# Second attention of a two-block transformer kernel: the queries' norm left out of the rotation and put into the exponentials and the row maxima, the norm weights put into tables and copies, and the first two score groups issued earlier

## What is computed

```python
qkv = u @ w_in
q = qkv[..., :1024].reshape(B, S, 16, 64)
k = qkv[..., 1024:1280].reshape(B, S, 4, 64)
v = qkv[..., 1280:].reshape(B, S, 4, 64)
q = partial_rope_2(rms_norm_2(q, q_gain), cos, sin)
k = partial_rope_2(rms_norm_2(k, k_gain), cos, sin)
scores = einsum(q, k) * (64 ** -0.5)            # masked to the window
probs = softmax(concat([scores, sink]))[..., :-1]
out = einsum(probs, v).reshape(B, S, 1024) @ w_out
```

## Time and profile before

| | |
|---|---|
| median of 3 runs | 1316.03 us (1315.31 to 1316.38) |
| profiled execution, its own time | 1316.13 us |
| its span | 1314.3 us |
| busy: PE / DVE / ACT / POOL | 98% / 75% / 55% / 8% of the span |
| second attention, projection and groups | about 545.5 to 609.6 us of the span |

### The profile page before, as it was taken

How to read it: one execution, slowest core, us unless ns; L and a number is a source line. 1 busy time by engine, 2 the same in 40 slices (tenths; PEclk the granted TensorE clock), 3 DMA queues, 4 the chain that set the end, 5 groups by cost and what they waited for, 6 DMA issues and landing times.

```text
span 1314.3 us, 21966 instructions
## 1 busy us (share of the span) xinstructions
PE 1291.2 (98%) x8296; PEld 1144.0 (87%) x8296; DVE 980.7 (75%) x1628; ACT 727.7 (55%) x1175; POOL 100.9 (8%) x95
## 2 busy tenths in 40 slices
PE   7999999999999999999999999999999999999998
PEld 6888889998888888987888888899998888888887
DVE  6866677767687666787776666899887975766666
ACT  5444446656554444675665555677653545655553
POOL 1000000000000000130000000013202820000000
PEclk9999999999999999999999999999999999999999
DMA  8655555720365555323355555454431123555552
GB/s 302 210 204 187 188 185 177 256 97 1 113 210 206 191 191 192 131 95 129 133 188 191 191 191 192 161 164 165 163 120 65 66 94 131 193 192 191 191 192 96
DMA packets 30600, 214.80 MB, mean 163 GB/s; under 512 B 3648, under 2 KB 3776, under 8 KB 5184
## 3 DMA queue, kind: packets, MB, share of 16 engines
q1 hardware_dynamic: 30096, 212.23, 45.9%
q0 software_dynamic: 432, 1.57, 0.4%
HBM read 212.74 MB, written 1.05 MB: 163 GB/s over the span
## 4 chain that ended last, share of the span: by engine, by line
PE 89%; DVE 6%; ACT 2%; issue 2%; DMA 1%; POOL 0%; SPq 0%; POOLq 0%; DVEq 0%; ACTq 0%
PE bank L508 25%; PE bank L669 24%; PE bank L503 19%; PE bank L705 5%; PE bank L496 5%; PE bank L884 1%; PE bank L934 1%; PE bank L903 1%; DVE w_lo L2216 1%; ACT w_hi L1486 1%; DVE aT L2451 1%; PE bank L561 1%; PE bank L1125 1%; DMA raw<-weights 1%; PE bank L1360 0%
## 5 line engine op out<-in xcount | busy, mean ns | idle before, releaser
L2216 DVE TENSOR_TENSOR w_lo<-raw,w_hi 128x2048 fp32r<-128x2048 f32 x151 | 348.6, 2310 | 110.9 <-ACT w_hi L1486 110.5
L1486 ACT ACTIVATE w_hi<-raw 128x2048 fp32r<-128x2048 f32 x198 | 377.9, 1910 | 69.1 <-PE bank L508 34.7
L669 PE MATMUL bank<-aT,w_hi 128*128 128x512 f32 x1424 | 340.4, 390 | 0.7 <-DVE aT L2243 0.6
L669 PEld LDWEIGHTS bank<-aT,w_hi 128*128 128x128 f32 x1424 | 263.6, 188 | 54.5 <-DVE aT L2243 1.4
L508 PEld LDWEIGHTS bank<-aT,w_lo 128*128 128x128 f32 x1664 | 212.4, 191 | 7.0
L508 PE MATMUL bank<-aT,w_lo 128*128 128x256 f32 x1664 | 215.9, 283 | 0.0
L503 PE MATMUL bank<-w_hi,hT_hi 128*128 128x512 f32 x400 | 156.5, 391 | 0.0
L508 PE MATMUL bank<-w_lo,hT_hi 128*128 128x512 f32 x400 | 151.9, 389 | 0.0
L705 PE MATMUL bank<-w_hi,hT_lo 128*128 128x512 f32 x322 | 125.3, 389 | 0.0
L503 PE MATMUL bank<-w_hi,aT 128*128 128x256 f32 (+1 forms) x736 | 119.0, 313 | 0.4 <-DVE aT L2243 0.2
L2224 DVE TENSOR_TENSOR w_lo<-raw,w_hi 128x1024 fp32r<-128x1024 f32 x95 | 115.5, 1218 | 1.6 <-ACT w_hi L1486 1.6
(11 more groups left out here) (395 smaller groups left out, 1730.7 us busy)
## 6 DMA issues: line engine op xcount, KB each, us to landing
raw<-weights SPq DMA_DIRECT2D x198, 1024.0 KB, 4.9
post_gain<-post_gains POOLq DMA_DIRECT2D x3, 512.0 KB, 4.2
residual<-x SPq DMA_DIRECT2D x2, 512.0 KB, 4.0
raw<-weights SPq DMA_DIRECT2D x2, 512.0 KB, 7.3
out<-residual SPq DMA_DIRECT2D x2, 512.0 KB, 2.6
par<-params SPq DMA_DIRECT2D x1, 809.0 KB, 11.1
con<-consts SPq DMA_DIRECT2D x1, 520.0 KB, 11.1
con<-consts SPq DMA_DIRECT2D x1, 64.0 KB, 4.2
```

Source lines behind the costliest of these rows:

```text
L669: nc.tensor.matmul(to[part][:, :], w, aT[:, k, :, :].rearrange("p a c -> p (a c)"), start=k == 0, stop=False)
L1486: nc.scalar.activation(w_hi[:, i % 3, :], raw[:, i % 3, :], ACT.Copy).then_inc(w_hi_done, 1)
L2216: nc.vector.tensor_tensor(w_lo[:, i % 3, :], raw[:, i % 3, :], w_hi[:, i % 3, :].bitcast(f32), ALU.subtract).then_inc(w_lo_done, 1)
```

## The change

Six edits, all for the second attention:

- The norm weights of queries and keys are no longer a pass over the block (L2665 is gone). For the 16 rotated dimensions they are multiplied into the sine and cosine tables once (eight small DVE operations in `set_up_tables`, results in `gain_tables`); for the others they become the per-partition factor of the copy of the transposed heads (`copy_heads` takes `scale` from `P("qk_column")` in place of a constant; two memsets put 1 at the rotated dimensions, a third operation puts the 1/8 in).
- The queries are rotated without their own norm: the pass L2667 stays for the keys alone.
- The norm is applied later: each exponential takes the query's norm as its per-partition `scale` (beside the bias), and each row maximum is multiplied by it (a new small DVE operation in `maximum`).
- PE issues score groups 0 and 1 inside item 5, and its low products for t = 1 and the last two transposes behind them.
- ACT takes the exponentials of group 0 ahead of `copy_block` of the values, and copies heads 1 and 2 earlier, on either side of the square of block 3.
- DVE takes the maximum of group 0 ahead of the last rotation.

```diff
@@ PE, attention_projection
-                project_rows(i, 5, 0)
+                high_rows(i, 5, 0)
                 turn_heads("att_in", 2, [3, 7])
-                project_rows(i, 5, 1).then_inc(item_done, 1)
+                low_ready(i)
+                low_rows(i, 5, 0, False)
                 pe.wait_ge(heads_copied, 10)
                 pe.wait_ge(copied, 15)
                 scores("att_in", 0)
+                high_rows(i, 5, 1, False)
+                pe.wait_ge(copied, 16)
+                scores("att_in", 1)
+                low_rows(i, 5, 1).then_inc(item_done, 1)
                 turn_heads("att_in", 3, [3, 7])
                 turn_heads("att_in", 4, [3, 7])
-
-                pe.wait_ge(copied, 16)
-                scores("att_in", 1)
                 pe.wait_ge(heads_copied, 12)
                 pe.wait_ge(copied, 17)
@@ ACT, copy_heads
+                scale = scales[b]
+                if layer == "att_in":
+                    scale = P("qk_column")[:, b == 0:(b == 0) + 1]
...
-                    nc.scalar.activation(heads[:, at:at + 2, :], source, ACT.Copy, scale=scales[b])\
+                    nc.scalar.activation(heads[:, at:at + 2, :], source, ACT.Copy, scale=scale)\
@@ ACT, attention_projection
                     if p == 5:
-                        copy_heads("att_in", 2, [3, 7])
+                        exponentials("att_in", 0)
                     copy_block("att_in", i, p, block)
+                    if p == 4:
+                        copy_heads("att_in", 1, [3, 7])
...
+                        if p == 4:
+                            copy_heads("att_in", 2, [3, 7])
                         split(i + 3)
-                    if p in (3, 4):
-                        copy_heads("att_in", p - 3, [3, 7])
+                    if p == 3:
+                        copy_heads("att_in", 0, [3, 7])
                 copy_heads("att_in", 3, [3, 7])
                 copy_heads("att_in", 4, [3, 7])
-                exponentials("att_in", 0)
                 exponentials("att_in", 1)
@@ ACT, exponentials
+                                                scale=query_rstd_column(n, c) if layer == "att_in" else 1.0,
@@ DVE, attention_projection
-                        gain = P("qk_gain")[:, 64 * (block == 4):64 * (block == 4) + 64]
-                        link(nc.vector.tensor_tensor(v, v, spread(spread(gain, 4, 1), 2, 1), ALU.mult))
-                        dve.wait_ge(head_normed, p)
-                        link(nc.vector.tensor_tensor(v, v, spread(r, 64, 3), ALU.mult))
-                        rope(block, cos_sin[:, 0:2, :], cos_sin[:, 2:4, :])
-                maximum("att_in", 0)
+                        if p == 1:
+                            dve.wait_ge(head_normed, 1)
+                            link(nc.vector.tensor_tensor(v, v, spread(r, 64, 3), ALU.mult))
+                        at = 16 * (block == 4)
+                        rope(block, [gain_tables[:, a, at:at + 16].rearrange("p (t c) -> p t c", t=2) for a in range(4)])
+                    if p == 4:
+                        maximum("att_in", 0)
                 maximum("att_in", 1)
@@ DVE, maximum
+                    if n in (0, 2):
+                        dve.wait_ge(head_normed, 3 + n)
+                    r = query_rstd(n)
+                    link(nc.vector.tensor_tensor(to.rearrange("p (j b) -> p j b", j=2) if count == 4 else to,
+                                                 to.rearrange("p (j b) -> p j b", j=2) if count == 4 else to, r, ALU.mult))
                     last = nc.vector.tensor_tensor(to, to, neg_sinks[:, h0:h0 + count], ALU.min)
@@ DVE, set_up_tables
+                cos, sin = cos_sin[:, 0:2, :], cos_sin[:, 2:4, :]
+                for side in range(2):
+                    gain = P("qk_gain")[:, 64 * side:64 * side + 16]
+                    for a, (angle, g) in enumerate(((cos, gain[:, 0:8]), (sin, gain[:, 8:16]),
+                                                    (cos, gain[:, 8:16]), (sin, gain[:, 0:8]))):
+                        nc.vector.tensor_tensor(gain_tables[:, a, 16 * side:16 * side + 16].rearrange("p (t c) -> p t c", t=2),
+                                                angle, spread(g, 2, 1), ALU.mult)
+
+                for rows in (slice(0, 16), slice(64, 80)):
+                    last = nc.vector.memset(P("qk_column")[rows, :], 1.0)
+                link(last)
+                nc.vector.tensor_scalar(P("qk_column")[:, 0:1], P("qk_column")[:, 0:1], 0.125, None, ALU.mult)
```

More of the change, by code:

```diff
@@ L33 @@
 LEVELS = [32, 64]
-PARAMS = {"gains": 56, "subln": 1, "gdn_norm": 1, "gdn_conv": 128, "ffn_conv": 144, "ffn_bias": 48, "a_log": 16,
+PARAMS = {"gains": 56, "subln": 1, "gdn_norm": 1, "qk_column": 2, "gdn_conv": 128, "ffn_conv": 144, "ffn_bias": 48, "a_log": 16,
           "dt_bias": 16, "pe": 32, "w2k": 256, "w2v": 128, "lambdas": 256, "qk_gain": 128, "sinks": 16, "small": 448}
@@ L169, in two_blocks @@
         used[0] = shared_at
+        gain_tables = rot[:, :, 192:224]
         v_pad = room(2, 2, 320)
@@ L398, in nsa_scale, with query_rstd, query_rstd_column @@
             return P("subln") if k < 4 else C("ones")[:, 0:1]
+        def query_rstd(n):
+            t, h0, count = GROUPS["att_in"][n]
+            r = head_rstd.rearrange("p (b t j a) -> p b t j a", b=5, t=2, j=2)[:, :, t, :, h0 // 4 % 2]
+            r = r[:, 1 + h0 // 8 * 2:3 + h0 // 8 * 2, :].rearrange("p b j -> p j b")
+            return r if count == 4 else r[:, h0 % 4 // 2, :]
+        def query_rstd_column(n, c):
+            t, h0, _ = GROUPS["att_in"][n]
+            q = HEADS["att_in"][h0 + c][0]
+            at = 8 * (1 + q // 2) + 4 * t + 2 * (q % 2) + h0 // 4 % 2
+            return head_rstd[:, at:at + 1]
         def squares_of(p):
@@ L1717, in copy_heads @@
                 act.wait_ge(keys_zeroed, 1)
-                nc.scalar.activation(to[0][0:64], source[0:64], ACT.Copy, scale=scales[b])
-                nc.scalar.activation(to[1][64:128], source[64:128], ACT.Copy, scale=scales[b])\
+                low, high = (scale[0:64], scale[64:128]) if layer == "att_in" else (scale, scale)
+                nc.scalar.activation(to[0][0:64], source[0:64], ACT.Copy, scale=low)
+                nc.scalar.activation(to[1][64:128], source[64:128], ACT.Copy, scale=high)\
                     .then_inc(heads_copied, 1)
@@ L2570, in ffn, with rope @@
                 ffn_order(dve, name, tile, down)
-            def rope(b, cos, sin):
+            def rope(b, tables):
                 v = proj[:, :, 256 * b:256 * b + 256].rearrange("p t (h d) -> p t h d", d=64)
@@ L2577, in rope @@
                 parts = [rot[:, a, at:at + 64].rearrange("p (t h d) -> p t h d", t=2, d=8) for a in range(4)]
-                cos, sin = spread(cos, 4, 2), spread(sin, 4, 2)
-                for to, a, c in zip(parts, (x1, x2, x2, x1), (cos, sin, cos, sin)):
-                    last = nc.vector.tensor_tensor(to, a, c, ALU.mult)
+                for to, a, c in zip(parts, (x1, x2, x2, x1), tables):
+                    last = nc.vector.tensor_tensor(to, a, spread(c, 4, 2), ALU.mult)
                 link(last)
@@ L2605, in mixer_projection @@
                         dve.wait_ge(copied, projections(p) + 1)
-                        rope(b, table[:, 0], table[:, 1])
+                        rope(b, [table[:, 0], table[:, 1], table[:, 0], table[:, 1]])
                     if p == 0:
@@ L3241, in _parameters @@
         "gdn_norm": a["gdn_norm_2"][0].reshape(128, 1),
+        "qk_column": _np.tile(_np.stack([a["attn_q_gain_2"].reshape(64), a["attn_k_gain_2"].reshape(64)], 1), (2, 1)),
         "gdn_conv": taps(a["gdn_conv_2"][0]),
```

## The result

Nine executions of the changed kernel have their median at 1320.26 us (1318.27 to 1320.53), against 1316.03 us for the kernel before: 1.0027 times as long, 95% interval 1.0019 to 1.0036. In a second session seven more gave 1318.74 us (1318.26 to 1320.28), 1.0026 (1.0015 to 1.0037). Both medians hide that there are two groups of times with nothing between them: eight of the sixteen executions lie from 1318.26 to 1318.94, the other eight from 1319.92 to 1320.53. The kernel before shows no such pair: 107 executions from 1315.31 to 1317.31. The profiled execution took 1318.94 us (span 1317.1), from the lower group: 2.81 us more than that of before. I explain first those 2.8 us, then the second group.

A forecast was written before the change was run, and what follows sets the result against it. PE was taken to bound the kernel, with only 2.4 us of early stalls to win. Terms 1.16 + 0.10 + 0.59 + 0.39 = 2.24 us on 1316.13 gave 1318.4, less 0.1 to the median 1318.3; range 1316.2 to 1319.7.

The forecast's parts named there:

- Slower by over 0.2%: Outcome class for the whole kernel, made up of the tipping or set-up case and the table-load case: chance 0.33.
- tipping loop: Rival: costlier product and operands leave the steady ACT loop 0.13 short each two groups; +3.0, 1319.1; 0.32 with set-up.
- uncovered set-up: Rival: the tables' set-up in the feed-forward layer ahead is not hidden; +1.1, 1319.5; chance 0.32 shared with tipping.
- table load: Rival: ACT's switch between copies, exponentials and square puts one 1.28 us load on the path; 1319.6, chance 0.01.
- Group 2 starts late, second transpose 585.4, +1.16: Score group 2 waits for head copies until 580.4, 1.6 late; second transpose of exponentials moves from 584.24 to 585.4.
- Operand 0.095, product 0.20: Each per-partition operand of an ACT operation costs 0.095 us; the new small DVE product in the maximum costs 0.20.
- additions are hidden: Rival: operands and product cost nothing, only the late group 2 remains; +0.4, 1316.4, chance 0.11.
- Steady loop +0.10, half split +0.59, last group +0.39: Second attention's three later places, where the added product and operands lengthen the ACT and DVE chains by these us.
- Set-up costed at nothing: About 1.1 us of added DVE table operations in the feed-forward layer ahead, taken as covered by a full PE.
- The parameter columns: Two more columns of parameters in the first DMA, claimed to cost nothing.
- The sum as work alone: Stage terms added as lengths of work and waits: 2.24 us, with nothing behind taking it back.

The follow-up runs named there:

- order_only: Changed kernel's instruction order with the arithmetic of the kernel before (both passes back, constant scales, no product), parameter columns kept: 1316.76 us.
- no_operand: Changed kernel with the exponentials' scale left at constant 1, so without the queries' norm there: 1317.87 us.
- no_product: Changed kernel without the small DVE product in the row maximum: five of ten executions 1317.38 to 1317.85 us, five 1319.21 to 1319.74.
- layout_only: Kernel before with only the two extra parameter columns, loaded and used by nobody: 1316.71 us against 1315.98.
- long_pause: Changed kernel with two more unused ACT copies lengthening PE's wait ahead of the second transpose: 1321.06, 1321.11, 1321.12 and 1322.39 us.
- fill: Changed kernel with unused matmuls in PE's waits, 4 ahead of score group 2 and 8 ahead of the second transpose: 1318.46 us.
- mended: Changed kernel's arithmetic, last head transposes and copies early, transposed-exponentials copy ahead of exponentials n + 2, 16 parameter columns: 1314.71 us, 0.9992 of before.

## Why the prediction was right and where it was wrong

I forecast 1318.3 us, range 1316.2 to 1319.7. The median of nine, 1320.26, lies above that range; the lower group and the second session's median lie inside. Five of the nine fell in the upper group: with one fewer the median would have been 1318.94, so on which side of my bound it came out was luck. "Slower by over 0.2%" came true, and I had given it 0.33 where I gave 0.59 to no measurable difference; but those 0.33 stood for a tipping loop, an uncovered set-up and a table load, and none of the three happened.

That the lower group (median 1318.5) lies so near to 1318.3 is luck in part too: my sum of 2.24 us for the stage was 0.35 too high (1.9 measured), and a term that I had put at nothing cost 0.7.

- *Group 2 starts late, second transpose 585.4, +1.16*: group 2 began at 580.33 (forecast 580.4), the second transpose at 585.37, with waits of 1.22 and 2.21 us where I named 1.5 and 2.2. Without the 0.20 that was there before the stage the term is 0.9. What I had too high is group 2's start: PE began 0.05 us behind the end of the head copies (579.01 + 1.27 = 580.28, 580.33), where I took 0.15. Of the 0.9, the late start by itself is only 0.2 (*order_only*).
- *Operand 0.095, product 0.20*: the two-head exponential takes 0.56 us (0.47 before), the head copy 94 ns more, the product stands 0.20 ahead of the minimum. The rival "additions are hidden" is refuted by *no_operand* and *no_product*.
- *Steady loop +0.10, half split +0.59, last group +0.39*: measured 0.04, 0.56 and 0.38. The loop did not tip.
- *Set-up costed at nothing*: right (PE 22.10 of 22.10). *Table loads*: L1826 follows L1734 without one (580.15 behind 579.01 + 1.27 on ACT).
- *The parameter columns: "nothing"*: this step failed. The columns alone cost 0.7 us, shown by *layout_only*; the loss is not at the first transfer but in the gated delta layer, where GpSimd's multiplies take longer, and with 16 columns in place of 2 it is gone.
- *The sum as work alone*: this step failed too. I priced PE's waits by their length, and took one of 1.25 us to 2.2 us without asking what the clock does in it. The clock is in none of my rivals. The upper group lies about 1.8 us above the lower in half of the executions, and it moves the median out of the range.

That the clock falls in such a wait, some 2.2 us into it, is shown in the profile of *long_pause*. For the changed kernel itself no execution of the upper group was profiled; there the cause rests on *fill* and on the table of waits. The granted clock averaged over these executions (0.998 to 0.999, the lower group's 0.999 to 1.000) says little. The profiled execution is of the lower group and has 0.999 as well, and it loses that in the last 1.7 us of its span, behind the last matmul:

```profile
1315.40:1317.10 1.70, 0.00 (x0) 0.00 (x0) 0.00 (x0) 0.00 (x0) 0.00 (x0) 0.52 0.49 200
```

Open is what decides between the groups of one kernel, and which operand's address makes GpSimd's multiply slower.

## What to carry to other kernels

Ask of each wait that a change lengthens not only how long it is but whether it is now long enough for PE's clock to fall: here a kernel with a wait of 1.85 us paid its length, and one with 2.01 us took nearly two us more in half of its executions. The work taken off DVE in a stretch where PE was full was worth nothing, while 0.1 or 0.2 us put on the short chain between scores and values was paid at every place where PE waited for that chain. An added column in a packed tensor moves everything behind it: compare the durations of unchanged operations before and after.

## What the runs showed of the hardware

- The granted clock fell some 2.2 us into a single PE wait of 3.2 us, behind a stretch at full clock, and the stretch at 1.2 GHz then lasted 6.8 us (*long_pause*). Of kernels with a wait of 2.0 to 2.4 us 17 of 37 executions were in an upper group, whose median lies 1.7 to 2.0 us above the lower's.
- Matmuls with unused results, in a time in which PE waits anyway, took the second group away at no cost (1318.46).
- Two more columns (8 bytes per partition) ahead of the other tensors lengthened GpSimd multiplies of 128x512 by 0.18 us (1087 to 1268 ns, 2461 to 2639 ns, *layout_only*); 16 columns (64 bytes) did not (1090 and 2464 ns, *mended*).
- A DVE operation on eight columns ended 0.03 us behind the GpSimd multiply that ran beside it, and so took 0.78 us in the one layout and 1.14 in the other; a DVE reduction beside GpSimd took 1.26 us in both.
- The mean granted clock of an execution can fall to 0.999 in its last 1.7 us, where no matmul is left to be slowed.
